# Stick-breaking attention: the minimum in front of the exponential issued from GpSimd in place of VectorE

## The chip, the core and the metric

The kernel is one program on one core of a Trainium2 chip. It computes a whole forward pass (one block with two attentions and a mixture of experts, then two hybrid layers) in float32. Time is device time in microseconds of one execution on that core; the figure is the median of several runs.

The names used below are the profile's: PE is TensorE (matrix products, PEld its weight loads), DVE is VectorE, ACT is ScalarE, POOL is GpSimd, SP issues the DMAs.

## The reference, cut to what matters

Each of the two hybrid layers contains a causal stick-breaking attention of 8 heads of 64 channels over 1024 positions:

```python
z = einsum('bhqd,bhsd->bhqs', qi, k) * scale
log_beta = log_sigmoid(z)
log_keep = where(mask, log_sigmoid(-z), 0.0)
suffix = cumsum(log_keep, axis=3, reverse=True) - log_keep
a = where(mask, exp(log_beta + suffix), 0.0)
out = einsum('bhqs,bhse->bhqe', a, v)
```

The kernel writes soft(z) = log(1 + exp(z)) for -log_sigmoid(-z). With T the sum of soft(z) over this key and all later allowed keys, the weight is exp(z - T). For large z the exponential would overflow, so the kernel computes soft(z) = max(z, log(1 + exp(min(z, 40)))). The `min(z, 40)` is the instruction that this change is about.

## The kernel before, in words

`stick_breaking_phase` runs twice, once in each hybrid layer. Between its start and its end nothing else of the program runs on the core. The work is cut into units `(pair, half, s)`: a pair of heads, a half of the 1024 queries (512 columns for each of the two heads, so tiles of 128 partitions x 2 x 512), and a block of 128 keys `s`, counted down. A half with s on the diagonal needs only the columns from the diagonal on, so the first units of each half are narrow. One pair has 12 units, whose tiles have 256, 512, 768, 1024, 1024, 1024, 1024, 1024 columns (half 1), and 256, 512, 768, 1024 (half 0), both heads counted. There are four pairs, hence 48 units in a phase.

A unit n passes through these steps, each with its own semaphore:

- `score(n)` on PE: the scores into one of two PSUM buffers.
- `copy_z(n)` on ACT (L2382): PSUM to `z[n % 3]`; signals `copied`.
- `cap(n)` on DVE (L2457): `soft[n % 2] = min(z, 40)`; signals `capped`.
- `exp(n)` (L2388) and `log(n)` (L2394) on ACT, in place in `soft`.
- `soften(n)` on DVE: `soft = max(z, soft)` (L2462), then the first head's rounded copy into `hi` (L2466).
- `high(n)` on ACT (L2401): the second head's rounded copy into `hi`; signals `hi1_done`.
- `split(n)` on DVE (L2471): `lo = soft - hi`; signals `lo_done`.
- `add_up(n)` on PE (L2308 with `hi`, L2312 with `lo`): the running sum T, by a product with a triangle of ones.
- `weigh(n)` on DVE (L2478): `w = z - T`; `weights(n)` on ACT (L2406): `exp(w)`.
- `multiply(n)` on PE (L2335): the product with the values; `carry(n)` (L2322) brings the sum on to the next key block.

Each engine works its own queue strictly in the order in which the code below issues it. ACT's order for a unit n is exp(n+1), log(n+1), copy_z(n+2), weights(n), high(n+1), and in four of the 12 units of a pair a `take` (L2374) of the next pair's turned queries or keys. DVE's order is weigh(n), soften(n+1), cap(n+2), split(n+1), then in the same four units a `lower` (L2449). `soft` has two buffers, so cap(n+2) writes the buffer that unit n used; its last readers are high(n) on ACT and split(n) on DVE. The second of these needs no wait as long as cap stands behind it on the same engine.

In both phases POOL has no work in this kernel; its DMAs belong to the dense stages before and after.

Of the kernel before, what the change touches and what calls it, by code (L numbers as in the profile page):

```python
# [10 lines left out]
ALU = mybir.AluOpType  # L11
# [57 lines left out]
def load_early(engine, k, w, first):  # L69

    engine.dma_start(k.early[:], w[:, first * CH:(first + 1) * CH].rearrange("(k p) n -> p k n", p=P)).then_inc(k.early_loaded, 16)
    k.early_loads += 1
# [2089 lines left out]
Z_TOP = 40.0  # L2162


def stick_breaking_phase(nc, k, tag, proj, dst, consts, after):
# [4 lines left out]
    N = len(UNITS)  # L2170
    PER = N // (HS // 2)
    with ExitStack() as stack:
# [4 lines left out]
        z = [s_.sb(f"z{p}", [P, 2, CH]) for p in range(3)]  # L2177
        soft, w = ([s_.sb(f"{n}{p}", [P, 2, CH]) for p in range(2)] for n in ("soft", "w"))
# [11 lines left out]
        con_done, turned, taken, lowered, scored, copied, capped, exped, logged, softed = (s_.sem(n) for n in (  # L2190
            "con_done", "turned", "taken", "lowered", "scored", "copied", "capped", "exped", "logged", "softed"))
        hi0_done, hi1_done, lo_done, summed, carried, weighed, w_done, product, o_taken, o_turned, y_done = (s_.sem(n) for n in (
            "hi0_done", "hi1_done", "lo_done", "summed", "carried", "weighed", "w_done", "product", "o_taken", "o_turned", "y_done"))
        block = s_.block()

        def part(ap):
            return ap.rearrange("(t p) d -> p t d", p=P)

        def off(n):

            return max(P * UNITS[n][2] - CH * UNITS[n][1], 0)

        def cols(n):
            return slice(off(n), CH)
# [15 lines left out]
        def misc(n):  # L2220


            pair, place = n // PER, n % PER
            if place in (3, 4, 5, 6) and pair + 1 < HS // 2:
                return "turn", pair + 1, place - 3
            if place == 9:
                return "rows", 2 * pair, None
            if place == 1 and pair > 0:
                return "rows", 2 * pair - 1, None
            return None  # L2230
# [13 lines left out]
        def wait_split_free(engine, n):  # L2244

            if last(n):
                engine.wait_ge(summed, n + 1)
            else:
                engine.wait_ge(carried, carries_upto(n))

        @block.sync
        def _(sp):
            def load(pair):
                for i in (1, 0):
                    first_col = S0 + i * SB + pair * 2 * DS
                    sp.dma_start(raw[i][:], part(proj[:, first_col:first_col + 2 * DS])).then_inc(loaded[i], 16)

            load(0)
            for i, of in enumerate(consts):
                sp.dma_start(con[:, i, :], of).then_inc(con_loaded, 16)  # L2260
            sp.dma_start(v[:], part(proj[:, S0 + 2 * SB:S0 + 3 * SB])).then_inc(v_loaded, 16)
            sp.wait_ge(turned, 4)
            load(1)
            sp.dma_start(g[:], part(proj[:, S0 + 3 * SB:S0 + 4 * SB])).then_inc(g_loaded, 16)
            load_early(sp, k, *after)
            for i in range(HS):
                pair, half = i // 2, 1 - i % 2
                if i % 2 and pair + 2 < HS // 2:
                    sp.wait_ge(turned, 4 * (pair + 2))
                    load(pair + 2)  # L2270
                sp.wait_ge(y_done, i + 1)
                tiles, ch = slice(4 * half, 4 * half + 4), slice(pair * 2 * DS, (pair + 1) * 2 * DS)
                sp.dma_start(part(dst[:, Y0:Y0 + SB])[:, tiles, ch], y[:, tiles, ch]).then_inc(stored, 16)
            sp.wait_ge(stored, 16 * HS)

        @block.tensor
        def _(pe):
            def turn(pair, group, bank):
# [161 lines left out]
        @block.vector  # L2440
        def _(dve):
            def lower(pair, group, bank):
                b = 1 - group % 2
                dve.wait_ge(taken, 4 * pair + group + 1)
                if pair >= 2:
                    dve.wait_ge(scored, PER * (pair - 1))
                to, of = ((k_lo, k_hi), (q_lo, q_hi))[group // 2]
                half = slice(b * CH, (b + 1) * CH)
                dve.scalar_tensor_tensor(out=to[pair % 2][:, half], in0=bank, scalar=1.0 if group < 2 else DS ** -0.5,  # L2449
                                         in1=of[pair % 2][:, half].bitcast(F), op0=ALU.mult, op1=ALU.subtract).then_inc(lowered, 1)  # L2450

            def cap(n):
                if n < N:
                    dve.wait_ge(copied, n + 1)
                    if n >= 2:
                        dve.wait_ge(hi1_done, n - 1)
                    dve.tensor_scalar(soft[n % 2][:, :, cols(n)], z[n % 3][:, :, cols(n)], Z_TOP, None, ALU.min).then_inc(capped, 1)  # L2457

            def soften(n):
                ap = soft[n % 2][:, :, cols(n)]  # L2460
                dve.wait_ge(logged, n + 1)
                dve.tensor_tensor(ap, z[n % 3][:, :, cols(n)], ap, ALU.max).then_inc(softed, 1)  # L2462
                dve.wait_ge(softed, n + 1)
                if n >= 2:
                    wait_split_free(dve, n - 2)
                dve.tensor_copy(hi[n % 2][:, 0, cols(n)], soft[n % 2][:, 0, cols(n)]).then_inc(hi0_done, 1)  # L2466

            def split(n):
                dve.wait_ge(hi0_done, n + 1)
                dve.wait_ge(hi1_done, n + 1)  # L2470
                dve.tensor_tensor(lo[n % 2][:, :, cols(n)], soft[n % 2][:, :, cols(n)], hi[n % 2][:, :, cols(n)].bitcast(F),  # L2471
                                  ALU.subtract).then_inc(lo_done, 1)

            def weigh(n):
                dve.wait_ge(summed, n + 1)
                if n >= 2:
                    dve.wait_ge(product, n - 1)
                dve.tensor_tensor(w[n % 2][:, :, cols(n)], z[n % 3][:, :, cols(n)], psT[:, :, cols(n)], ALU.subtract).then_inc(weighed, 1)  # L2478

            def rows(i):  # L2480
                pair, half = i // 2, 1 - i % 2
                dve.wait_ge(o_turned, i + 1)
                if i == 0:
                    dve.wait_ge(g_loaded, 16)
                tiles, ch = slice(4 * half, 4 * half + 4), slice(pair * 2 * DS, (pair + 1) * 2 * DS)
                dve.tensor_tensor(y[:, tiles, ch], psM.rearrange("p (t d) -> p t d", d=P), g[:, tiles, ch], ALU.mult).then_inc(y_done, 1)

            for group in range(4):
                lower(0, group, psZ[group // 2][:, group % 2, :])
            cap(0)  # L2490
            soften(0)
            cap(1)
            split(0)
            for n in range(N):
                weigh(n)
                if n + 1 < N:
                    soften(n + 1)
                cap(n + 2)
                if n + 1 < N:
                    split(n + 1)  # L2500
                if misc(n) is not None:
                    if misc(n)[0] == "turn":
                        lower(misc(n)[1], misc(n)[2], psM)
                    else:
                        rows(misc(n)[1])
            rows(HS - 1)
# [134 lines left out]
```

## Time and profile before

| | us |
|---|---|
| median of 3 runs | 3345.75 (3343.57 to 3347.57) |
| the profiled execution | 3348.34 |
| its span | 3346.8 |
| first stick-breaking phase, first copy of scores to last product | about 2196 to 2422 |
| second one | about 2994 to 3216 |
| PE, DVE, ACT, POOL busy over the span | 2880.2, 1545.8, 1221.4, 316.3 |

The span is what the profile covers; the execution's own time is 1.5 us longer. Shares over the whole span say little of these two phases, in which DVE and ACT are far busier than on the mean. An instruction row gives its start (us from the span's start), its duration, the engine, the line, the tile written and those read, and the shapes; in brackets stands the idle time of the engine ahead of it and what ended it.

### The profile page before, as it was taken

The numbers are of one execution on the slowest core, as the hardware profiler recorded it, in microseconds if no ns is written. First come the engines' busy times: TensorE is split into PE (matmuls) and PEld (weight loads), VectorE is DVE, ScalarE is ACT, GpSimd is POOL, SyncE is SP. The second block draws the span as 40 slices with busy tenths as digits, with TensorE's granted clock in tenths as the row PEclk, the third lists the DMA queues.
The fourth block names the chain that finished last, engine by engine and source line by source line (L and its number), as shares of the span: only waits on it lengthen the run. The fifth ranks groups of instructions, "written<-read, shape, count | busy, mean of one in ns | idle before, by whom it ended". The sixth has DMA issues, their size and how long they took to land. (4 is left out here: it accounts for less than half of the span.)

```text
span 3346.8 us, 60156 instructions
## 1 busy us (share of the span) xinstructions
PE 2880.2 (86%) x22510; PEld 2232.3 (67%) x22510; DVE 1545.8 (46%) x2937; ACT 1221.4 (36%) x2232; POOL 316.3 (9%) x475
## 2 busy tenths in 40 slices
PE   7997896888869999999589999778788999868878
PEld 5786664666638878777467888644476888754446
DVE  3862786885242222222445310368744421058854
ACT  3332564774131100000523212368723222148841
POOL 0001561000021222221000000000000000000000
PEclk9998997999889999999799999879998999989989
DMA  5213664112459999999652221440064222260035
GB/s 175 80 72 105 192 176 143 38 38 86 151 200 356 376 376 377 379 377 359 210 196 93 97 100 47 136 131 23 13 206 139 98 97 75 82 194 19 26 113 182
DMA packets 241572, 530.39 MB, mean 158 GB/s; under 512 B 27760, under 2 KB 110640, under 8 KB 216720
## 3 DMA queue, kind: packets, MB, share of 16 engines
q1 hardware_dynamic: 214464, 458.11, 38.3%
q0 software_dynamic: 25808, 70.07, 7.4%
q8 instruction: 89, 1.46, 0.2%
q14 instruction: 59, 0.48, 0.0%
q10 hardware_dynamic: 1152, 0.27, 0.0%
HBM read 425.15 MB, written 104.15 MB: 158 GB/s over the span
## 5 line engine op out<-in xcount | busy, mean ns | idle before, releaser
L544 PE MATMUL ps<-wh,in_xh 128*128 (+1 forms) x1024 | 402.6, 393 | 0.0
L546 PE MATMUL ps<-wh,in_xl 128*128 (+1 forms) x1024 | 400.4, 391 | 0.0
L545 PE MATMUL ps<-wl,in_xh 128*128 (+1 forms) x1024 | 400.4, 391 | 0.0
L545 PEld LDWEIGHTS ps<-wl,in_xh 128*128 128x128 f32 x1024 | 194.0, 189 | 40.3
L544 PEld LDWEIGHTS ps<-wh,in_xh 128*128 128x128 f32 x1024 | 194.0, 189 | 39.8
L546 PEld LDWEIGHTS ps<-wh,in_xl 128*128 128x128 f32 x1024 | 193.4, 189 | 40.5
L533 PE MATMUL ps<-ident,x 128*128 128x128 f32 x416 | 69.4, 319 | 128.0 <-DVE x L376 59.5
L1143 DVE TENSOR_TENSOR ex_hid<-ps,ex_act 32x128 f32<-32x128 f32 x96 | 28.2, 294 | 312.0 <-PE ps L1194 311.2
L544 PE MATMUL ps<-mix_in_wh,mix_in_xh 128*128 (+1 forms) x384 | 151.9, 396 | 9.1 <-DVE mix_in_out L442 5.6
L533 PEld LDWEIGHTS ps<-ident,x 128*128 128x128 f32 x416 | 56.9, 164 | 143.4 <-DVE x L376 63.7
L546 PE MATMUL ps<-mix_in_wh,mix_in_xl 128*128 (+1 forms) x384 | 149.9, 390 | 0.0
L545 PE MATMUL ps<-mix_in_wl,mix_in_xh 128*128 (+1 forms) x384 | 149.8, 390 | 0.0
L365 DVE TENSOR_TENSOR wl<-early,wh x80 | 54.0, 688 | 166.7 <-ACT wh L262 166.7
L294 ACT COPY in_out<-ps 128x512 f32<-128x512 f32 x64 | 37.6, 588 | 248.8 <-PE ps L546 248.8
L232 POOL DMA_DIRECT2D x<-y x4 | 2.1, 528 | 1282.4 <-POOLq L36 1282.4
L1152 DVE COPY ex_y<-ps 32x256 f32<-32x256 f32 x96 | 41.0, 427 | 171.0 <-PE ps L1221 160.6
L365 DVE TENSOR_TENSOR wl<-in_raw,wh (+1 forms) x64 | 44.1, 689 | 159.8 <-ACT wh L262 159.8
L2478 DVE TENSOR_TENSOR stick_w<-stick_z,ps 128x256 f32<-128x256 f32 (+2 forms) x96 | 91.6, 954 | 50.9 <-PE ps L2312 49.4
L1192 PE MATMUL ps<-ex_w_w1b,ex_xT 128*32 128x384 f32 x768 | 88.8, 488 | 17.0 <-DMA ex_w_w1b<-in_w_dram 17.0
L1105 ACT COPY ex_xT<-ps 128x768 f32<-128x768 f32 x33 | 26.4, 799 | 204.7 <-PE ps L1173 204.7
L2471 DVE TENSOR_TENSOR stick_lo<-stick_soft,stick_hi 128x256 fp32r<-128x256 f32 (+2 forms) x96 | 91.6, 954 | 15.4 <-ACT stick_hi L2401 13.9
L2406 ACT ACTIVATE stick_w<-stick_w 128x256 f32<-128x256 f32 (+2 forms) x96 | 81.4, 848 | 45.5 <-DVE stick_w L2478 41.7
(415 smaller groups left out, 7357.7 us busy)
## 6 DMA issues: line engine op xcount, KB each, us to landing
ex_w_w1a<-in_w_dram SPq DMA_DIRECT2D x32, 1024.0 KB, 14.6
ex_w_w1b<-in_w_dram SPq DMA_DIRECT2D x32, 1024.0 KB, 15.7
ex_w_w3a<-in_w_dram SPq DMA_DIRECT2D x32, 1024.0 KB
ex_w_w3b<-in_w_dram SPq DMA_DIRECT2D x32, 1024.0 KB, 15.5
ex_w_w2a<-in_w_dram SPq DMA_DIRECT2D x32, 1024.0 KB, 15.6
ex_w_w2b<-in_w_dram SPq DMA_DIRECT2D x32, 1024.0 KB
proj<-in_out SPq DMA_DIRECT2D x128, 256.0 KB, 2.0
da_w_ada<-in_w_ada_dram SPq DMA_DIRECT2D x32, 768.0 KB, 4.5
```

Of the source, the lines that this page charges most:

```text
L294: act.copy(out[p][:], k.ps[:, 2 + p, :]).then_inc(out_ready, 1)
L365: dve.tensor_tensor(wl[:, c % 2, bass.ds(kt, 1), :], raw[c % 2][:, bass.ds(kt, 1), :], wh[:, c % 2, bass.ds(kt, 1), :].bitcast(F), ALU.sub ...
L533: last = pe.transpose(psT[p][:, kt * P:(kt + 1) * P], x[p][:, kt * P:(kt + 1) * P], k.ident[:])
L544: pe.matmul(o, xh[:, kt, tok], wb[0], start=(kt == 0), stop=False)
L545: pe.matmul(o, xh[:, kt, tok], wb[1], start=False, stop=False)
L546: last = pe.matmul(o, xl[:, kt, tok], wb[0], start=False, stop=(kt == KT - 1))
L1143: dve.tensor_tensor(hid[group(g), HM:], psH[1][BR:P, g * HQ:(g + 1) * HQ], act1[BR:P, g * HQ:(g + 1) * HQ], ALU.mult)
L1152: dve.tensor_copy(y[group(g), YM:], psY[BR:P, g * YQ:(g + 1) * YQ])
L1192: pe.matmul(o[group(g), :], tokens[g], wh[j][:, q, 0:HM], start=first, stop=end)
L2406: act.activation(ap, ap, ACT.Exp).then_inc(w_done, 1)
L2471: dve.tensor_tensor(lo[n % 2][:, :, cols(n)], soft[n % 2][:, :, cols(n)], hi[n % 2][:, :, cols(n)].bitcast(F), ALU.subtract).then_inc(lo_d ...
L2478: dve.tensor_tensor(w[n % 2][:, :, cols(n)], z[n % 3][:, :, cols(n)], psT[:, :, cols(n)], ALU.subtract).then_inc(weighed, 1)
```

## The change

`cap` leaves DVE's queue. A new POOL program issues the same instruction for all 48 units in order. POOL waits for `copied` (z is there), and, from the third unit on, for both readers of the `soft` buffer that it overwrites: `hi1_done` as before, and `lo_done`, which DVE's own order gave before. On DVE `split(n+1)` now stands right behind `soften(n+1)`. All other queues are issued as they were.

```diff
+        @block.gpsimd
+        def _(pool):
+            for n in range(N):
+                pool.wait_ge(copied, n + 1)
+                if n >= 2:
+                    pool.wait_ge(hi1_done, n - 1)
+                    pool.wait_ge(lo_done, n - 1)
+                pool.tensor_scalar(soft[n % 2][:, :, cols(n)], z[n % 3][:, :, cols(n)], Z_TOP, None, ALU.min).then_inc(capped, 1)
...
-            def cap(n):
-                if n < N:
-                    dve.wait_ge(copied, n + 1)
-                    if n >= 2:
-                        dve.wait_ge(hi1_done, n - 1)
-                    dve.tensor_scalar(soft[n % 2][:, :, cols(n)], z[n % 3][:, :, cols(n)], Z_TOP, None, ALU.min).then_inc(capped, 1)
...
-            cap(0)
             soften(0)
-            cap(1)
             split(0)
             for n in range(N):
                 weigh(n)
                 if n + 1 < N:
                     soften(n + 1)
-                cap(n + 2)
-                if n + 1 < N:
                     split(n + 1)
```

DVE's queue in the middle of a half, before the change, one full unit (the row at L2457 is `cap`):

```order
L2478 TENSOR_TENSOR stick_w<-stick_z,ps 128x1024
L2462 TENSOR_TENSOR stick_soft<-stick_z,stick_soft 128x1024
L2466 CAST stick_hi<-stick_soft 128x512
L2457 TENSOR_SCALAR stick_soft<-stick_z 128x1024
L2471 TENSOR_TENSOR stick_lo<-stick_soft,stick_hi 128x1024
L2449 SCALAR_TENSOR_TENSOR stick_k_lo<-ps,stick_k_hi 128x512
```

The same place of the changed kernel (its lines are numbered otherwise: L2481 is `weigh`, L2465 and L2469 `soften`, L2474 `split`, L2459 `lower`):

```order
L2481 TENSOR_TENSOR stick_w<-stick_z,ps 128x1024
L2465 TENSOR_TENSOR stick_soft<-stick_z,stick_soft 128x1024
L2469 CAST stick_hi<-stick_soft 128x512
L2474 TENSOR_TENSOR stick_lo<-stick_soft,stick_hi 128x1024
L2459 SCALAR_TENSOR_TENSOR stick_k_lo<-ps,stick_k_hi 128x512
```

One row of six has gone; nothing else moved on DVE. On POOL, ahead of the DMAs of the next dense stage, this now stands at the start of each phase:

```order
L2276 UNCONDITIONAL_BRANCH
L2284 TENSOR_SCALAR stick_soft<-stick_z 128x2x128
L2284 TENSOR_SCALAR stick_soft<-stick_z 128x2x256
L2284 TENSOR_SCALAR stick_soft<-stick_z 128x2x384
L2284 TENSOR_SCALAR stick_soft<-stick_z 128x1024 x5
```

The pattern goes on through the 48 units; they are the only instructions in POOL's queue during a phase.

## Rows read from the trace of the kernel before

**Rows 1.** Busy time by engine over one pair of heads in the first phase.
```profile
core 0: us, PE busy (x) PEld busy (x) DVE busy (x) ACT busy (x) POOL busy (x), PEclk, DMA share, GB/s
2265.00:2319.00 54.00, 47.15 (x250) 26.06 (x249) 46.48 (x67) 46.27 (x67) 0.00 (x0) 1.00 0.11 30
```
**Rows 2.** ScalarE in order of time, over one pair of heads.
```profile
2263.88 1.06 ACT L2388 ACTIVATE stick_soft<-stick_soft 128x1024 f32<-128x1024 f32 x1 [0.48 <-DVE stick_soft L2457]
...
2273.99 1.06 ACT L2388 ACTIVATE stick_soft<-stick_soft 128x1024 f32<-128x1024 f32 x1
...
2276.04 1.00 ACT L2382 COPY stick_z<-ps 128x1024 f32<-128x1024 f32 x1
2277.16 1.06 ACT L2406 ACTIVATE stick_w<-stick_w 128x1024 f32<-128x1024 f32 x1
2278.30 0.62 ACT L2401 CAST stick_hi<-stick_soft 128x512 fp32r<-128x512 f32 x1
2278.85 0.60 ACT L2374 ACTIVATE stick_k_hi<-ps 128x512 fp32r<-128x512 f32 x1
...
2284.74 1.06 ACT L2388 ACTIVATE stick_soft<-stick_soft 128x1024 f32<-128x1024 f32 x1
...
2290.10 0.41 ACT L2388 ACTIVATE stick_soft<-stick_soft 128x256 f32<-128x256 f32 x1
...
2294.23 0.63 ACT L2388 ACTIVATE stick_soft<-stick_soft 128x512 f32<-128x512 f32 x1
...
2295.43 0.78 ACT L2382 COPY stick_z<-ps 128x768 f32<-128x768 f32 x1
...
2297.50 0.84 ACT L2388 ACTIVATE stick_soft<-stick_soft 128x768 f32<-128x768 f32 x1
...
2299.13 1.00 ACT L2382 COPY stick_z<-ps 128x1024 f32<-128x1024 f32 x1
...
2301.57 1.06 ACT L2388 ACTIVATE stick_soft<-stick_soft 128x1024 f32<-128x1024 f32 x1 [0.48 <-DVE stick_soft L2457]
...
2317.77 1.06 ACT L2388 ACTIVATE stick_soft<-stick_soft 128x1024 f32<-128x1024 f32 x1 [0.48 <-DVE stick_soft L2457]
```
**Rows 3.** VectorE in order of time, one full unit.
```profile
2277.05 1.22 DVE L2462 TENSOR_TENSOR stick_soft<-stick_z,stick_soft 128x1024 f32<-128x1024 f32 x1
2278.30 0.43 DVE L2466 CAST stick_hi<-stick_soft 128x512 fp32r<-128x512 f32 x1
2278.64 0.69 DVE L2457 TENSOR_SCALAR stick_soft<-stick_z 128x1024 f32<-128x1024 f32 x1
2279.24 1.22 DVE L2471 TENSOR_TENSOR stick_lo<-stick_soft,stick_hi 128x1024 fp32r<-128x1024 f32 x1
2280.38 0.68 DVE L2449 SCALAR_TENSOR_TENSOR stick_k_lo<-ps,stick_k_hi 128x512 fp32r<-128x512 f32 x1
2281.29 1.22 DVE L2478 TENSOR_TENSOR stick_w<-stick_z,ps 128x1024 f32<-128x1024 f32 x1 [0.23 <-PE ps L2312]
```
**Rows 4.** GpSimd's arithmetic elsewhere in the program, in order of time.
```profile
490.02 1.01 POOL L1369 TENSOR_TENSOR da_m_row<-da_m_row,da_m_bias 128x384 f32<-128x384 f32 x1
491.12 1.16 POOL L1371 TENSOR_SCALAR da_m_gained<-da_m_row 128x384 f32<-128x384 f32 x1
...
906.50 0.39 POOL L675 COPY rt_wr<-rt_w_expert 128x256 f32<-128x256 f32 x1
```
**Rows 5.** The instructions of two lines, min/median/max in ns: GpSimd's other tensor-scalar, and VectorE beside POOL.
```profile
L1623 POOL TENSOR_SCALAR da_rpb<-da_rpb x1: 1411/1411/1411, 324.7 to 324.7; 16x465 f32<-16x465 f32 x1
...
L1547 DVE SCALAR_TENSOR_TENSOR da_coef<-da_inv,da_total,da_neg_lam x32: 219/219/984, 340.8 to 528.6; 128x1 f32<-128x1 f32 x32
...
L1550 DVE SCALAR_TENSOR_TENSOR da_w<-da_e,da_coef x32: 1283/1284/1611, 341.0 to 528.9; 128x1024 f32<-128x1024 f32 x32
```
**Rows 6.** VectorE in order of time, beside the rows of GpSimd above.
```profile
490.38 0.67 DVE L1547 SCALAR_TENSOR_TENSOR da_coef<-da_inv,da_total,da_neg_lam 128x1 f32<-128x1 f32 x1
491.09 1.61 DVE L1550 SCALAR_TENSOR_TENSOR da_w<-da_e,da_coef 128x1024 f32<-128x1024 f32 x1
```

## The prediction, made before the changed kernel ran

> **What bounds the kernel now.** I read the page's 40 slices first: POOL is idle in both stick-breaking phases while DVE and ACT are at their busiest, so the change puts work on an idle engine. The windows say how full the others are: over one pair of heads, 54 us, DVE is busy 46.5 us and ACT 46.3 us, PE's granted clock is 1.00, POOL does nothing [rows 1]. No engine is full. Two loops of waits stand side by side, and the question is what each holds and which becomes the longer.
>
> The first loop is on DVE: soften, the rounded copies, cap, split, the product on PE, weigh, soften of the next unit. In a full unit (1024 columns) soften starts at 2277.05 and weigh at 2281.29, DVE idling only 0.23 us in between [rows 3]. One turn of it is 5.38 us: two steps from 2273.99 to 2284.74 [rows 2]. Take cap out of it and split could start when ACT's `high` ends, at 2278.30 + 0.62 = 2278.92, where today it starts at 2279.24 [rows 2, 3]; with a handoff of 0.05, that is 0.27 us.
>
> The second loop is on ACT: exp, log, copy_z, then cap on the copied z, then exp of that unit. Today cap is hidden: between the end of copy_z (2277.04) and the next exp ACT has weights (1.06), high (0.62) and in some units a take (0.60) [rows 2], and DVE's cap of 0.69 [rows 3] fits beside them. It shows only as a wait of 0.48 us ahead of the exp of the first full unit of a half [rows 2].
>
> **The price of the moved instruction.** The change issues 96 caps on POOL: 48 with 1024 columns and 16 each with 256, 512 and 768. The trace has no POOL minimum and no POOL tensor-scalar of 1024 columns. It has two others: 384 columns with 128 partitions in 1.16 us [rows 4] and 465 columns with 16 partitions in 1.41 us [rows 5], both 3.03 ns a column. So a full cap is 1024 x 3.03 = 3.10 us (2.33 for 768, 1.55 for 512, 0.78 for 256) against 0.69 on DVE. Bounds: POOL's two-input sum of 384 columns took 1.01 us, 2.62 ns a column or 2.68 us; POOL's plain copy of 256 columns took 0.39 us [rows 4], 1.54 ns a column, 1.58 us at that rate, and, if half of its time is a fixed part, near 1 us. That is the lower end. I take 3.10, because a tensor-scalar is what those two rows are.
>
> The GPSIMD Engine Reference of the Trainium skill, section 4.1, says the other thing: two-input operations are about 2x slower than on VectorE, but one-input ones run roughly at line rate; section 3.1 gives 1.03 cycles per element for light bodies, an estimate of 0.88 us for 1024 columns. By that the cap would stay hidden and the kernel would be a little faster. The trace's two one-input tensor-scalars, at 3.03 ns a column, do not agree, while the plain copy at 1.54 lies between.
>
> **What lies on the path.** ACT's step from exp to exp is at least: exp start to copy_z start, copy_z of the next unit, handoff to POOL 0.10 (the gap between two dependent POOL instructions, 491.03 to 491.12 [rows 4]), the cap, handoff back 0.05 (estimate). For full units: 2.05 (2273.99 to 2276.04) + 1.00 + 0.10 + 3.10 + 0.05 = 6.30 us. Weights, high and take (2.28 together) now lie beside the cap. The wait for `lo_done` costs nothing itself: split(n) ends before weigh(n) starts, and copy_z(n+2), for which cap waits too, ends later. Behind the waiting exp on ACT stand log, copy_z, weights and high of the next unit, and for them wait DVE (soften, split) and PE. By size, against today [rows 2]:
> - 1024 to 1024, four a pair: 4 x 6.30 = 25.20 against 2284.74 - 2263.88 = 20.86: +4.34.
> - 768 to 1024, two a pair: 1.63 + 1.00 + 0.15 + 3.10 = 5.88 against 4.07 (2297.50 to 2301.57): 2 x 1.81 = +3.62. The second lies in 2301.57 to 2317.77 and repeats the first.
> - 512 to 768, two a pair: 1.20 + 0.78 + 0.15 + 2.33 = 4.46 against 3.27: 2 x 1.19 = +2.38.
> - 1024 to 256 and 256 to 512: the cap of 0.78 or 1.55 hides. The first loop sets these (5.36 and 4.13 in the first half). But in the slowed units that loop gains slack of about 1 us, so at 1024 to 256 weigh comes in time, and ACT's own work is left: 2.05 + 0.34 (copy of 256, from 1.00 and 0.78 going down by 0.22 a size) + 1.06 + 0.62 + 0.60 is about 4.6, so -0.75; about -0.3 in the other half, which has no take.
>
> Sum: 4.34 + 3.62 + 2.38 - 1.05 = 9.3 us a pair, eight pairs: +74. The 0.27 us that DVE saves lies in a loop that no longer ends last, and counts nothing. At the start of a phase copy_z(1) stands ahead of exp(0) and hides the first cap; nothing follows on POOL but the DMAs of the next stage, which start after the phase as now.
>
> **The port.** DVE and POOL get in each other's way in this trace. DVE's L1547 has a median of 0.22 us; begun at 490.38 beside POOL's two-input sum it takes 0.67 and ends at 491.05, just after the sum's end at 491.03 [rows 4 to 6]. Beside POOL's tensor-scalar (491.12, 384 columns) DVE's two-input L1550 takes 1.61 instead of 1.28 [rows 5, 6]: 0.33 us more, not 1.16. Scaled to 1024 columns, a cap takes the port for some 0.9 us, most of it while DVE has slack. The other way, soften (two SBUF inputs, 1.22) starts together with copy_z (1.00) and ends 0.2 later, so the cap may start its reads 0.1 to 0.2 late: 0 to 0.2 x 6 x 8 = 0 to 10 us. I take +4. Sum +78: 3348.3 + 78 = 3426 for the profiled execution, and on the median 3345.75 + 78 = 3424.
>
> **Rivals.**
> - *The port is held for the whole cap.* Then a cap that starts at T stops soften, which is ready while it runs, until T + 3.1; soften 1.22 and high 0.62 follow, then exp 1.06, log and copy_z (2.05 + 1.00) and the handoffs: 3.1 + 1.22 + 0.65 + 3.05 + 0.15 = 8.2 us a full step, 1.9 more than the forecast. 1.9 x 4 + about 1.9 x 2 = 11 a pair, 92 in all: 3424 + 92 = about 3515. For it: L1547 beside the two-input sum. Against it: the 0.33 us of L1550 beside the very kind of instruction that is added. The Trainium skill's SBUF page (SBUF — State Buffer, section "Who interferes with whom") states this rule, the shared pair locked for the whole instruction against a VectorE instruction with two SBUF inputs; the trace agrees for the sum and not for the tensor-scalar. 12%.
> - *The cap is quick: not slower.* If POOL's minimum runs as its copy, 1.0 to 1.6 us, it hides behind weights and high (1.68) and the full step is set by ACT and DVE again. DVE's loop gives 0.27 x 4 a pair, the 0.48 ahead of some exps is a gain or a small loss: 0 to -2 us a pair, -16 to 0: about 3337. It decides as soon as the full cap is under 5.38 - 3.20 = 2.2 us. For it: the copy. Against: both tensor-scalars. 15%, of which 10 faster and 5 no change.
> - *The change does nothing* because the minimum was hidden before and is again: the same case at caps near 1.7 to 2.2 us, about 3348; in the 15%, with 1% more.
>
> **The numbers.** The forecast holds 72%. Its own range: at 2.68 us a full cap the steps give 2.66 + 2.78 + 1.74 - 1.05 = 6.1 a pair, +49, 3395; with a port wait of about 0.9 us in each of the six full steps of a pair, +43 on 3424, 3467. The range for 8 in 10 leaves out the quick cap and the longer half of the locked port: 3375 to 3500. What can be told from no change here is about 0.2%, 6.7 us. Faster 0.10, same 0.06, slower 0.84.
>
> **What the changed profile would show.** Right: POOL rows of about 3.1 us for 1024 columns; ACT idle ahead of exp with POOL as releaser, 0.8 us and more in most full units; exp to exp 6.3 us in full units; cap gone from DVE and DVE idle longer, waiting for ACT's log; soften at most 0.9 us longer than 1.22. Wrong: a full cap under 2.2 us (quick cap); soften or split of 3 to 4 us (locked port); the narrow steps growing too; or a granted PE clock well under 1.00 in the middle of the phases, which this sum leaves out.

## The result, and the profile after

The changed kernel takes 3403.76 us (median of 4 runs, 3402.19 to 3409.53) against 3344.66 of the kernel before, run beside it: a ratio of 1.018, 95% interval 1.0168 to 1.0193, or 59 us more. The forecast was 3424, own range 3395 to 3467. The profiled execution took 3402.24 with a span of 3400.7. The two phases carry the growth: from the first copy of scores to the last copy of the output the first one lasted 224.2 us before (2196.56 to 2420.74) and 253.4 after (2196.50 to 2449.89), the second 223.2 (2994.45 to 3217.64) and 251.8 (3020.57 to 3272.34); 57.8 us together. (The profiled executions differ by 53.9 us, 3402.24 against 3348.34: the rest of the program was 3.9 us shorter in the one after.)

ScalarE after, in order of time, over one pair of heads (L2398 is `exp`, L2392 `copy_z`, L2416 `weights`, L2411 `high`; the rows answer to [rows 2]):

```profile
2271.46 1.06 ACT L2398 ACTIVATE stick_soft<-stick_soft 128x1024 f32<-128x1024 f32 x1 [1.96 <-POOL stick_soft L2284]
2272.55 1.06 ACT L2404 ACTIVATE stick_soft<-stick_soft 128x1024 f32<-128x1024 f32 x1
2273.51 1.00 ACT L2392 COPY stick_z<-ps 128x1024 f32<-128x1024 f32 x1
2274.40 0.84 ACT L2416 ACTIVATE stick_w<-stick_w 128x768 f32<-128x768 f32 x1
2275.15 0.61 ACT L2411 CAST stick_hi<-stick_soft 128x512 fp32r<-128x512 f32 x1
2277.52 1.06 ACT L2398 ACTIVATE stick_soft<-stick_soft 128x1024 f32<-128x1024 f32 x1 [1.77 <-POOL stick_soft L2284]
...
2283.63 1.06 ACT L2398 ACTIVATE stick_soft<-stick_soft 128x1024 f32<-128x1024 f32 x1
...
2290.30 1.06 ACT L2398 ACTIVATE stick_soft<-stick_soft 128x1024 f32<-128x1024 f32 x1 [1.47 <-POOL stick_soft L2284]
...
2296.37 1.06 ACT L2398 ACTIVATE stick_soft<-stick_soft 128x1024 f32<-128x1024 f32 x1 [1.05 <-POOL stick_soft L2284]
...
2300.82 0.41 ACT L2398 ACTIVATE stick_soft<-stick_soft 128x256 f32<-128x256 f32 x1
...
2304.99 0.62 ACT L2398 ACTIVATE stick_soft<-stick_soft 128x512 f32<-128x512 f32 x1
...
2309.20 0.84 ACT L2398 ACTIVATE stick_soft<-stick_soft 128x768 f32<-128x768 f32 x1 [0.85 <-POOL stick_soft L2284]
...
2314.71 1.06 ACT L2398 ACTIVATE stick_soft<-stick_soft 128x1024 f32<-128x1024 f32 x1 [1.96 <-POOL stick_soft L2284]
```

ACT now stands idle ahead of nearly every exp of a wide unit, and the releaser is POOL: 88.8 us ahead of 70 of the 96 exps, where before DVE's cap held up 34 of them for 15.2 us. One chain can be read off: exp starts at 2271.46, copy_z ends at 2274.51, POOL's cap starts at 2274.59 and takes 2.90 (next fence), exp starts at 2277.52. That is 6.06 us for a full step, where 5.38 was usual before. From the first of these rows to the same place of the next pair (2333.05) it is 61.59 us; before it was 53.89 (2263.88 to 2317.77 [rows 2]). 7.70 x 8 pairs = 61.6, a little over the 57.8 measured, since the pairs differ: in the first phase the part ahead of the first full unit's exp grew by 1.6 us, then the four pairs by 6.1, 7.7, 8.3 and 5.5, the last of which has no narrow units of a next pair behind it.

GpSimd after, in order of time, over the same pair:

```profile
2268.66 2.77 POOL L2284 TENSOR_SCALAR stick_soft<-stick_z 128x1024 f32<-128x1024 f32 x1 [2.74 <-ACT stick_z L2392]
2274.59 2.90 POOL L2284 TENSOR_SCALAR stick_soft<-stick_z 128x1024 f32<-128x1024 f32 x1 [3.16 <-ACT stick_z L2392]
...
2286.76 3.50 POOL L2284 TENSOR_SCALAR stick_soft<-stick_z 128x1024 f32<-128x1024 f32 x1 [3.16 <-ACT stick_z L2392]
...
2298.86 1.70 POOL L2284 TENSOR_SCALAR stick_soft<-stick_z 128x256 f32<-128x256 f32 x1 [2.52 <-ACT stick_z L2392]
2302.23 1.49 POOL L2284 TENSOR_SCALAR stick_soft<-stick_z 128x512 f32<-128x512 f32 x1 [1.67 <-ACT stick_z L2392]
2307.04 2.13 POOL L2284 TENSOR_SCALAR stick_soft<-stick_z 128x768 f32<-128x768 f32 x1 [3.32 <-ACT stick_z L2392]
```

All 96 caps were released by copy_z, none by the readers of soft. Undisturbed caps take 1.49, 2.13 and 2.77 us for 512, 768 and 1024 columns (0.84 for 256, the shortest in the trace): 0.21 us and 2.50 ns a column. Caps that overlap with DVE's soften take longer: 2.90 is the mean of the 48 full ones.

VectorE after, one full unit (answers to [rows 3]; L2465 and L2469 are `soften`, L2474 `split`):

```profile
2273.64 1.23 DVE L2465 TENSOR_TENSOR stick_soft<-stick_z,stick_soft 128x1024 f32<-128x1024 f32 x1 [1.07 <-ACT stick_soft L2404]
2274.90 1.14 DVE L2469 CAST stick_hi<-stick_soft 128x512 fp32r<-128x512 f32 x1
2276.07 1.23 DVE L2474 TENSOR_TENSOR stick_lo<-stick_soft,stick_hi 128x1024 fp32r<-128x1024 f32 x1
```

The cap is gone, DVE waits for ACT's log, and the cast has grown from 0.43 to 1.14 while POOL's cap reads. soften started before the cap (2273.64 against 2274.59) and ended at 2274.87; the cap took 0.13 more than its 2.77.

### The profile page after: what moved, and what is told of

Same layout as the page of the kernel before. It is cut to its first block and busy times, and to the rows that moved or that the text cites. A ratio compares the mean times of both kernels' runs of the same rounds, so it can differ in the third digit from the quotient of the medians.

```text
span 3400.7 us, 60156 instructions
## 1 busy us (share of the span) xinstructions
PE 2906.2 (85%) x22510; PEld 2244.2 (66%) x22510; DVE 1556.5 (46%) x2841; ACT 1216.5 (36%) x2232; POOL 539.2 (16%) x571
## 5 line engine op out<-in xcount | busy, mean ns | idle before, releaser
L2284 POOL TENSOR_SCALAR stick_soft<-stick_z 128x256 f32<-128x256 f32 (+2 forms) x96 | 223.0, 2323 | 1079.6 <-ACT stick_z L2392 1079.6
L2481 DVE TENSOR_TENSOR stick_w<-stick_z,ps 128x256 f32<-128x256 f32 (+2 forms) x96 | 91.7, 955 | 57.9 <-PE ps L2322 57.0
L2398 ACT ACTIVATE stick_soft<-stick_soft 128x256 f32<-128x256 f32 (+2 forms) x96 | 81.0, 843 | 89.0 <-POOL stick_soft L2284 88.8
L2465 DVE TENSOR_TENSOR stick_soft<-stick_z,stick_soft 128x256 f32<-128x256 f32 (+2 forms) x96 | 91.8, 956 | 39.7 <-ACT stick_soft L2404 39.7
L2474 DVE TENSOR_TENSOR stick_lo<-stick_soft,stick_hi 128x256 fp32r<-128x256 f32 (+2 forms) x96 | 92.0, 959 | 23.0 <-ACT stick_hi L2411 21.2
L1192 PE MATMUL ps<-ex_w_w1b,ex_xT 128*32 128x384 f32 x768 | 88.8, 488 | 15.9 <-DMA ex_w_w1b<-in_w_dram 15.9
```

The costliest lines, as they stand in the source:

```text
L1192: pe.matmul(o[group(g), :], tokens[g], wh[j][:, q, 0:HM], start=first, stop=end)
L2284: pool.tensor_scalar(soft[n % 2][:, :, cols(n)], z[n % 3][:, :, cols(n)], Z_TOP, None, ALU.min).then_inc(capped, 1)
L2398: act.activation(ap, ap, ACT.Exp).then_inc(exped, 1)
```

## The experiments

Times are medians, beside the kernel before run on the same chip; ratios have 95% intervals. Line numbers of rows are those of each kernel.

**Another instruction on POOL, all else the same but exp's scale.** This kernel leaves the minimum out.

```diff
-                pool.tensor_scalar(soft[n % 2][:, :, cols(n)], z[n % 3][:, :, cols(n)], Z_TOP, None, ALU.min).then_inc(capped, 1)
+                pool.tensor_copy(soft[n % 2][:, :, cols(n)], z[n % 3][:, :, cols(n)]).then_inc(capped, 1)
...
-                    act.activation(ap, ap, ACT.Exp).then_inc(exped, 1)
+                    act.activation(ap, ap, ACT.Exp, scale=0.01).then_inc(exped, 1)
```

> The changed kernel, but POOL copies z into soft in place of taking the minimum: same columns, same waits, same bytes read and written. The minimum is left out of the computation, and exp takes 0.01 times its argument so that it stays finite. Theory 1 (the length of POOL's instruction sets the time, since copy_z, cap, exp and log stand in one loop): POOL's copy was 0.39 us for 256 columns elsewhere, so 0.9 to 1.6 us for 1024 against 2.8 to 2.9 of the minimum; the idle time of ACT ahead of exp (88.8 us in all) falls under 20, and the time comes back to 3340 to 3365. Theory 2 (handing the work to POOL and back, and the waits on both readers of soft, set the time): those are as in the changed kernel, 3395 to 3410. Theory 3 (POOL and DVE keep each other from the port): a copy reads as much as the minimum does, so most of the +59 stays, above 3385.

3357.98 against 3342.74, ratio 1.0043 (1.0027 to 1.0060): 44 of the 59 us are gone with the handoffs, waits and bytes unchanged. GpSimd and VectorE of this kernel, in order of time:

```profile
2266.41 1.04 POOL L2284 COPY stick_soft<-stick_z 128x1024 f32<-128x1024 f32 x1 [3.14 <-ACT stick_z L2392]
...
2287.61 0.61 POOL L2284 COPY stick_soft<-stick_z 128x512 f32<-128x512 f32 x1 [3.72 <-ACT stick_z L2392]
```
```profile
2277.87 1.04 POOL L2284 COPY stick_soft<-stick_z 128x1024 f32<-128x1024 f32 x1 [3.28 <-ACT stick_z L2392]
2278.10 1.89 DVE L2465 TENSOR_TENSOR stick_soft<-stick_z,stick_soft 128x1024 f32<-128x1024 f32 x1
```

A full copy takes 1.04 us undisturbed (1.31 on the mean of 48) and is nearly hidden: ACT waits for POOL 7.7 us in all. What is left, +15, has another source, the port, that is, what DVE and POOL keep each other from when both run: soften begun 0.23 us after the copy takes 1.89 instead of 1.22. Over the 48 full units soften takes 1.47 us on the mean, against 1.22 before, and the cast 0.61 against 0.43. DVE never waits for ACT's log ahead of a full soften here (in the changed kernel it does, 23.9 us in all), so it has no slack and the port counts.

**The wait for both readers taken away, by a third buffer.**

```diff
-                if n >= 2:
-                    pool.wait_ge(hi1_done, n - 1)
-                    pool.wait_ge(lo_done, n - 1)
+                if n >= 3:
+                    pool.wait_ge(hi1_done, n - 2)
+                    pool.wait_ge(lo_done, n - 2)
```

(with `soft[n % 3]` everywhere and three buffers)

> The changed kernel with three soft buffers in place of two: cap(n) then waits for high and split of unit n-3, a unit earlier than now. Theory 1 (length of the cap; the wait for both readers is always over when copy_z ends): 3404 within 7, full steps of ACT from exp to exp stay 6.1 us. Theory 2 (POOL's wait for both readers of the buffer is what costs): cap starts earlier, most of the +59 goes, 3345 to 3375.

3404.08 against 3342.74, ratio 1.0183 (1.0165 to 1.0202): as the changed kernel. ScalarE's exp of two neighbouring full units:

```profile
2275.61 1.06 ACT L2398 ACTIVATE stick_soft<-stick_soft 128x1024 f32<-128x1024 f32 x1 [1.77 <-POOL stick_soft L2284]
2281.67 1.06 ACT L2398 ACTIVATE stick_soft<-stick_soft 128x1024 f32<-128x1024 f32 x1 [1.05 <-POOL stick_soft L2284]
```

6.06 again. The wait for both readers costs nothing.

**The cap twice.**

```diff
+                pool.tensor_scalar(spare[:, :, cols(n)], z[n % 3][:, :, cols(n)], Z_TOP, None, ALU.min).then_inc(beside, 1)
+                pool.wait_ge(beside, n + 1)
                 pool.tensor_scalar(soft[n % 2][:, :, cols(n)], z[n % 3][:, :, cols(n)], Z_TOP, None, ALU.min).then_inc(capped, 1)
```

> The changed kernel with POOL's minimum issued twice in a row, first into a tile of its own that nobody reads. Theory 1 says by how much: each step of ACT into a full unit grows by one more cap, 2.8 to 2.9 us, 6 a pair; into a 768 unit by 2.2, 2 a pair; into a 512 unit by about 0.5 and into a 256 unit by 0 to 0.5, since those had room: 17.1 + 4.4 + 1 to 2 = about 23 a pair, eight pairs, +180 on 3404: 3565 to 3600, full steps 8.9 to 9.0 us. Theory 3 (port): the doubled reads hit DVE twice, no such regular growth; DVE's rows rather than POOL's length would carry it. Theory 2 (a fixed handoff): 3405 to 3420.

3602.81 against 3343.52, ratio 1.0776 (1.0759 to 1.0792): +199 on the changed kernel, 3 us above the range. One full step of it, in order of time:

```profile
2302.41 1.06 ACT L2401 ACTIVATE stick_soft<-stick_soft 128x1024 f32<-128x1024 f32 x1 [4.80 <-POOL stick_soft L2287]
...
2305.53 2.90 POOL L2285 TENSOR_SCALAR stick_spare<-stick_z 128x1024 f32<-128x1024 f32 x1 [3.16 <-ACT stick_z L2395]
2308.51 2.76 POOL L2287 TENSOR_SCALAR stick_soft<-stick_z 128x1024 f32<-128x1024 f32 x1
2311.31 1.06 ACT L2401 ACTIVATE stick_soft<-stick_soft 128x1024 f32<-128x1024 f32 x1 [4.61 <-POOL stick_soft L2287]
```

8.90 us a step, 2.84 more than 6.06: POOL's time adds to the step one for one. What the expectation had too small is the step from a full to a 256-column unit: it grew from 4.45 and 4.22 us in the two halves to 6.12, where 0 to 0.5 more had been expected.

**The port alone: POOL work beside the kernel before.**

```diff
+        @block.gpsimd
+        def _(pool):
+            pool.wait_ge(v_loaded, 16)
+            for n in range(N):
+                pool.wait_ge(copied, n + 1)
+                if n > 0:
+                    pool.wait_ge(beside, n)
+                pool.tensor_scalar(spare[:, :, cols(n)], v[:, 0:2, cols(n)], Z_TOP, None, ALU.min).then_inc(beside, 1)
```

> The kernel before (cap on DVE), with an instruction on POOL beside it that nobody waits for: it starts when copy_z(n) is done, as the moved cap does, is of the same size and kind, reads tile v and writes a tile of its own. It shows the port alone. Theory 1 (the loss of +59 is the cap's length in the loop): most of the loss is absent; what DVE loses is the first head's cast, 0.7 us longer in full units where DVE has only 0.2 us to spare, so 0.5 us in up to 48 full steps and less in the others, +10 to +35: 3353 to 3378. Theory 3 (the port is the cause of the +59): at least as much as in the changed kernel, 3400 or more.

3387.44 against 3343.52, ratio 1.0130 (1.0115 to 1.0146): +44, though nobody waits for POOL. That is 9 us above the range of theory 1, and less than theory 3 gave. Its rows in order of time:

```profile
2273.61 1.22 DVE L2472 TENSOR_TENSOR stick_soft<-stick_z,stick_soft 128x1024 f32<-128x1024 f32 x1
2273.68 3.82 POOL L2284 TENSOR_SCALAR stick_spare<-stick_v 128x1024 f32<-128x1024 f32 x1 [2.27 <-ACT stick_z L2392]
...
2274.87 1.14 DVE L2476 CAST stick_hi<-stick_soft 128x512 fp32r<-128x512 f32 x1
2275.93 0.68 DVE L2467 TENSOR_SCALAR stick_soft<-stick_z 128x1024 f32<-128x1024 f32 x1
...
2279.71 1.22 DVE L2472 TENSOR_TENSOR stick_soft<-stick_z,stick_soft 128x1024 f32<-128x1024 f32 x1
```

The cast is 0.71 us longer, and the step from soften to soften 6.10 instead of 5.38: the whole 0.71 goes into it. My expectation took DVE's 0.23 us ahead of weigh for slack. It is none: that idle time waits for PE, which waits for split, so it moves along. The 32 steps from a full unit to a full unit grew by 24 us in all, the 16 from 768 to 1024 columns by 9 (4.07 to 4.59 each) and the 16 from 512 to 768 by 5 (3.27 to 3.54). In ten steps, none of them among the first four of a phase, the granted PE clock was 0.57 to 0.83; some of these were longer still (6.80 us at 0.75), and that is in the 44 as well. POOL's own row, begun 0.07 us behind soften, is 3.82 us, 1.05 longer than 2.77, about what was left of soften.

**The order on ACT.** Three places for copy_z(n+2), with cap on POOL or on DVE. The early one:

```diff
+                copy_z(n + 2)
                 exp(n + 1)
                 log(n + 1)
-                copy_z(n + 2)
```

The middle one:

```diff
                 exp(n + 1)
+                copy_z(n + 2)
                 log(n + 1)
-                copy_z(n + 2)
```

> The changed kernel with one thing moved on ACT: copy_z(n+2) stands ahead of exp(n+1) and log(n+1) in place of behind them, so that the cap on POOL has these two (2.1 us) beside it as well. Theory 1 (the loop copy_z, cap, exp, log): the cap of 2.8 to 2.9 us is out of the path, as 2.1 + 1.7 us of ACT's work stand between the copy and the exp that needs it; the full step falls from 6.1 to about 5.1 to 5.5 us, time 3335 to 3360. Where below 3345 it would be by the 0.27 us a full step that DVE saves, and it is above by what the port costs DVE's loop (the first head's cast grew from 0.43 to 1.14 us in full units). Theory 3 (port): the cap now reads beside other DVE instructions but as much, so most of the +59 stays, above 3385.

> The kernel before (cap on DVE), with copy_z(n+2) ahead of exp(n+1) and log(n+1) on ACT, the same edit as in the run with the early copy, which came to +24 where up to +17 was expected. If the +24 is the price of the order on ACT (copy_z now stands between high and exp, in the loop of soften, high, copy_z, exp, log), it shows here too, without any POOL: 3360 to 3375. If it was what POOL's cap still costs, this kernel stays at 3335 to 3350.

> The changed kernel with copy_z(n+2) between exp(n+1) and log(n+1). The cap on POOL (2.77) then has log, weights and high beside it (1.06 + 1.06 + 0.62 = 2.74 and a take in some units), and starts its reads beside weigh, which takes one operand from PSUM. log ends 1.0 us later than now, which soften can just bear (in the kernel before it started 0.9 us after log's end). By theory 1 nearly all of the +59 comes back: 3335 to 3360; full steps 5.1 to 5.5 us and POOL's wait ahead of exp under 10 us in a phase. By theory 2 or 3 it stays above 3385. Under 3340 it would beat the kernel before.

> The kernel before (cap on DVE), with copy_z(n+2) between exp(n+1) and log(n+1) on ACT. The same edit on the changed kernel gave +20 over the kernel before, with POOL hardly waited for (4.9 us in the first phase). If the +20 is the price of that order on ACT (log, and with it soften, a unit's copy later), this kernel shows +10 to +25 too: 3353 to 3368. If it is the port (POOL's reads beside DVE's two-input instructions and casts), it stays within 5 of 3343.

| copy_z | cap on POOL | cap on DVE |
|---|---|---|
| behind log | 3403.76, 1.0180 (1.0168 to 1.0193) | 1 |
| ahead of exp | 3367.17, 1.0066 (1.0049 to 1.0083) | 3375.02, 1.0100 (1.0084 to 1.0115) |
| between exp and log | 3363.24, 1.0058 (1.0044 to 1.0072) | 3360.20, 1.0049 (1.0034 to 1.0065) |

Give POOL room and its cap costs no more than DVE's: with either other order the two columns lie within 0.4% of each other, where they were 1.8% apart. Both new orders are dearer than the old one by themselves, 31 and 18 us with cap on DVE; I had left that price out, and with cap on POOL the early copy missed its range by 7 us and the middle one by 3. Why the orders cost that was not taken apart. With cap on DVE and the early copy, 15 of the 31 us lie in the 14 steps from a full unit to the next half's or pair's first, six of which took 6.0 to 6.3 us at a granted PE clock of 0.64 to 0.71, where the kernel before never fell below 1.00 in them. In the middle order the caps begin ahead of soften, and all 48 full ones take 2.77 us (GpSimd of that kernel, then VectorE beside the first of these caps):

```profile
2276.00 2.77 POOL L2284 TENSOR_SCALAR stick_soft<-stick_z 128x1024 f32<-128x1024 f32 x1 [2.93 <-ACT stick_z L2392]
2281.21 2.77 POOL L2284 TENSOR_SCALAR stick_soft<-stick_z 128x1024 f32<-128x1024 f32 x1 [2.44 <-ACT stick_z L2392]
```
```profile
2276.90 1.23 DVE L2465 TENSOR_TENSOR stick_soft<-stick_z,stick_soft 128x1024 f32<-128x1024 f32 x1
2278.16 0.88 DVE L2469 CAST stick_hi<-stick_soft 128x512 fp32r<-128x512 f32 x1
```

**The minimum shared between POOL and DVE.**

```diff
+                pool.tensor_scalar(soft[n % 2][:, 1, cols(n)], z[n % 3][:, 1, cols(n)], Z_TOP, None, ALU.min).then_inc(capped1, 1)
...
+                    dve.tensor_scalar(soft[n % 2][:, 0, cols(n)], z[n % 3][:, 0, cols(n)], Z_TOP, None, ALU.min).then_inc(capped, 1)
```

> The minimum is shared: POOL takes the second head's columns, DVE the first head's in cap's old place in its queue; exp waits for both. Theory 1: POOL's part of a full unit is 512 columns, 1.49 us by the changed kernel's rows, and is hidden beside weights and high (1.68 us on ACT); the step is again set by DVE's and ACT's own work, time 3335 to 3360. Theory 2 (handoffs and waits): as many handoffs as in the changed kernel, 3390 to 3410. Theory 3 (port): half of the reads, about half of the loss, 3370 to 3380.

3349.28 against 3342.74, ratio 1.0016 (1.0006 to 1.0026). With copy_z in the middle as well:

> The shared minimum (POOL the second head, DVE the first) together with copy_z(n+2) between exp(n+1) and log(n+1). The wait of 0.4 us ahead of exp that the shared minimum left goes, since POOL starts 1.06 us earlier; against that log ends 1.0 later, and the port stays. From the two runs: +6 for the shares, +20 for the order with a whole cap on POOL, less the 15.7 us of waits a phase as far as they were in the loop: 3345 to 3365. Under 3340 it would beat the kernel before.

3343.74 against 3341.89, ratio 1.0003 (0.9994 to 1.0013): the interval holds no change, and the time is 1 us below the range. The first leaves a short wait in full units (POOL's part is longer than 1.49 beside soften and the cast):

```profile
2279.74 2.18 POOL L2285 TENSOR_SCALAR stick_soft<-stick_z 128x512 f32<-128x512 f32 x1 [3.22 <-ACT stick_z L2393]
```
```profile
2282.01 1.06 ACT L2400 ACTIVATE stick_soft<-stick_soft 128x1024 f32<-128x1024 f32 x1 [0.39 <-POOL stick_soft L2285]
```

**No minimum at all.**

```diff
-                    act.activation(ap, ap, ACT.Exp).then_inc(exped, 1)
+                    act.wait_ge(copied, n + 1)
+                    if n >= 2:
+                        act.wait_ge(lo_done, n - 1)
+                    act.activation(soft[n % 2][:, :, cols(n)], z[n % 3][:, :, cols(n)], ACT.Exp, scale=0.01).then_inc(exped, 1)
```

> No minimum at all, on no engine: exp reads z directly with a scale of 0.01 (so that it stays finite) and writes soft; it waits for split of the unit before the last in cap's place. The minimum is left out of the computation. This is the most that moving the cap off DVE could give, with a POOL that costs nothing. The waits for DVE's cap ahead of exp (15.2 us over both phases) go, and 0.27 us in full steps where ACT is not full: by the prediction's figures 0 to -25, 3320 to 3343. Were DVE's 0.69 us a unit the thing to win (the other view: cap on DVE costs its whole 53 us), it would be 3290 to 3300.

3333.69 against 3341.89, ratio 0.9972 (0.9961 to 0.9984). This is about all that a free POOL could have given in this order of the queues: 9 us by the ratio, 5 to 13 by its interval. No version that computes the minimum was measurably faster than the kernel before.

## Why the prediction was right, point by point

*What bounds the phases, and the loop of copy_z, cap, exp, log.* Right, and shown three ways: a shorter instruction on POOL gave back 44 us, twice the cap added 2.84 us to every full step, and room on ACT's queue took the difference between POOL and DVE away.

*The price of the cap.* This is the term that was too large; the time still fell inside the range, whose lower end, 3395, was worked out with a cap of 2.68 us. I scaled 1.16 us for 384 columns and 1.41 for 465 in proportion, 3.03 ns a column, 3.10 us. Measured: 0.21 us fixed and 2.50 ns a column, 2.77 us. The same line gives 1.17 for 384 columns, as the row of before had it. A row of a small instruction holds the fixed part, and scaling it up multiplies that too. The two rows at hand could not have told: 81 columns apart they differ by 0.25 us, which leaves nothing for a fixed part, and the one of 465 columns covers 16 partitions and lies 0.04 above the line (1.41 against 1.37). POOL's copy shows it again: 0.61 and 1.04 us for 512 and 1024 columns are 0.84 ns a column and 0.18 fixed, where 0.39 us for 256 had been read as up to 1.54 a column.

In the sum the price is worth 0.33 us for each of six full caps and 0.20 for each of two of 768 columns, 2.4 a pair and 19 in all, which is the distance from the 78 forecast to the 59 measured. That it comes out so exactly is luck: the smaller misses (the handoffs, the pairs at the ends of the phases, the clock below) go both ways and cancel.

*The steps.* With the measured price and the handoffs as the rows have them (0.08 us to POOL and 0.03 back, for 0.10 and 0.05) they come out: 2.05 + 1.00 + 0.08 + 2.90 + 0.03 = 6.06 for a full step, 1.63 + 1.00 + 0.11 + 2.77 = 5.51 from 768 to 1024, 1.20 + 0.78 + 0.11 + 2.13 = 4.22 from 512 to 768.

| step | forecast | measured |
|---|---|---|
| 1024 to 1024, four | 25.20 | 24.91 (2271.46 to 2296.37), of it 0.6 in a step at a low clock, see below |
| 768 to 1024 | 5.88 | 5.51 |
| 512 to 768 | 4.46 | 4.21 |
| 1024 to 256, first half | about 4.6 | 4.45 |
| 1024 to 256, second half | about 4.0 | 4.22 |
| growth of a pair | 9.3, and 0.5 for the port | 7.7 |

*The port.* The size in the changed kernel was about right: 0.13 us a full cap (2.90 against 2.77), against the 0.1 taken. The reason that it is small there is that the loop through POOL leaves DVE idle ahead of a full soften in most full steps, 0.35 us with the cast already at 1.14, and 1.07 in the step shown. In a kernel in which DVE sets the pace the same collision costs 44 us. The Trainium skill (SBUF — State Buffer, "Who interferes with whom") states that whoever issues first gets the shared pair for the whole instruction while the other fully blocks. The trace agrees that each engine delays the other, and not on how long: the cap begun at 2274.59 ran until 2277.49, and the cast begun at 2274.90 was over at 2276.04, 0.71 us late.

*The wait for `lo_done`.* Right: nothing, shown by the third buffer.

*The rival of a quick cap* fell to the instruction's length, not to the reasoning. With POOL's copy the cap is quick and hidden, but the kernel was still 15 us slower than before, where I had given that case -16 to 0: I had let it off the port. *The locked port* gave 8.2 us a full step; 6.06 was measured. *What DVE saves* was put at nothing, since its loop no longer ends last; without any minimum the ceiling is 9 us.

*Left out, and present:* a fall of the granted PE clock in the middle of the phases, which the prediction names among the signs that it is wrong. The windows of four full steps after:

```profile
2271.46:2277.52 6.06, 3.45 (x18) 1.79 (x18) 4.59 (x5) 4.26 (x5) 2.90 (x1) 0.94 0.14 43
2277.52:2283.63 6.11, 6.11 (x18) 3.36 (x20) 4.78 (x5) 5.07 (x6) 2.95 (x1) 0.51 0.00 0
2283.63:2290.30 6.67, 5.98 (x31) 3.05 (x28) 5.59 (x6) 5.13 (x6) 3.50 (x1) 1.00 0.00 0
2290.30:2296.37 6.07, 4.96 (x25) 2.67 (x26) 5.42 (x6) 4.98 (x7) 2.90 (x1) 1.00 0.00 0
```
```profile
2285.29 1.22 DVE L2481 TENSOR_TENSOR stick_w<-stick_z,ps 128x1024 f32<-128x1024 f32 x1 [1.01 <-PE ps L2322]
2286.42 1.22 DVE L2465 TENSOR_TENSOR stick_soft<-stick_z,stick_soft 128x1024 f32<-128x1024 f32 x1
```

(The columns are those of [rows 1].) PE was busy 3.45 of 6.06 us, then its clock stood at 0.51, the 1.2 GHz level, for a step; weigh came late (1.01 us of waiting for PE), soften with it, and the next cap, begun beside soften, took 3.50. The step was 6.67, 0.6 us more. Before, the clock was 1.00 over the whole pair [rows 1]. Leaving out the first four steps of each phase, most of which are at 0.50 in both kernels, 16 of 86 steps from exp to exp have a granted clock of 0.50 to 0.87 after, and none is below 1.00 before. Two of the steps grow to 6.6 us or more, a few narrower ones by 0.1 to 0.8. Against the same steps at 1.00 all this comes to about 3 us, an estimate: the sign was there, but it is not what the 59 us are made of.

## What to carry to other kernels

Before moving an instruction to an idle engine, write down the loop of waits it stands in and how much of other work lies between its input and its reader: here 1.7 to 2.3 us on ACT, and the instruction was 0.69 us on one engine and 2.77 on the other. What frees an engine gives only what that engine's own loop can use, 9 us here although 53 us of DVE's work went (24 x 2 full caps of 0.69 and the narrower ones). Price the instruction by rows well apart in size and of the same number of partitions, a fixed part and a slope, and remember that idle time which waits for one's own product is not slack.

## What the runs showed of the hardware that was not expected

- GpSimd's float32 tensor-scalar with a minimum costs three times its copy per column, 2.50 against 0.84 ns; both with 0.2 us fixed. VectorE takes 0.69 us for the same 1024 columns.
- In the collision of the two engines it matters who starts first, and only part of POOL's instruction counts: soften begun 0.07 us ahead of the cap kept its 1.22 us and the cap took 3.82; begun 0.23 us behind POOL's copy it took 1.89. The cast of 0.43 us behind soften took 1.14 or 1.15 with either POOL instruction beside it. In the middle order soften begun 0.90 us into the cap kept its 1.23 us, and the cast begun 0.61 us before the cap's end took 0.88 and was over 0.27 us after it. So the beginning and the end of a cap delay a cast; what each part of it holds is not shown.
- weigh, which has one operand in PSUM, kept its 1.22 us beside a cap begun 0.2 us ahead of it, as the early order shows:

```profile
2279.24 2.77 POOL L2284 TENSOR_SCALAR stick_soft<-stick_z 128x1024 f32<-128x1024 f32 x1 [2.81 <-ACT stick_z L2392]
2279.45 1.22 DVE L2481 TENSOR_TENSOR stick_w<-stick_z,ps 128x1024 f32<-128x1024 f32 x1 [0.22 <-PE ps L2322]
```
